# Feed-forward up-projections on TensorE: a high weight tile streams both parts of the activations in one matmul, and the first and last tiles get an order of their own

## The chip, the cores and the metric

The kernel runs on one core of a Trainium2 chip (eight cores in all, the other seven idle). The metric is the device time of one execution in microseconds; the number compared is the median of several executions.

## The reference, cut to what matters

The program is a chain of ten stages over 256 tokens of width 1024: a mixing layer, five feed-forwards and four other mixers. Only the feed-forwards change. Each is

```python
h = rmsnorm(x, g)                          # 256 x 1024
u = dwconv(h @ w_up, conv_w, conv_b)       # 256 x 5632, depthwise, 3 taps along the tokens
g, v = u[..., :D_FF], u[..., D_FF:]        # D_FF = 2816 = 22 tiles of 128
y = (gelu(g) * v) @ w_down                 # 256 x 1024
x = x + rmsnorm(y, g_post)
```

Everything is fp32. The kernel keeps this accuracy with two reduced fp32 parts of each operand, a high one (a copy in the type `F32R`) and a low one (the rest), and three products: high by high, low weight by high activation, high weight by low activation.

## The kernel before, in words

Weights arrive as one stream of 263 chunks of 128 x 2048 values (1 MB), in the order of use. SyncE loads chunk c into `raw`, a ring of 3 slots (`RING`), as soon as the low part of chunk c-3 has been made. ScalarE copies the chunk to `w_hi` (`split_hi`, L685, in the loop `loop_split`, L906) once TensorE has used chunk c-3; VectorE subtracts and writes `w_lo` (`split_lo`, L1171, in the loop L1491). TensorE waits for `lo_done`.

A feed-forward has 33 chunks: for each of 22 tiles of 128 inner channels an `up` chunk (gate and value columns of that tile, 8 blocks of 128 x 128 each), and for each pair of tiles one `down` chunk. The activations h lie transposed as 8 blocks of 128 x 256 in `h_hi` and `h_lo`.

TensorE (`ffn`, L2173): `up(t)` does 16 steps of three matmuls of 256 columns (`product`, L1988 to L1990) into one PSUM bank, gate in its left half and value in its right; three banks take turns. `down(i)` does 24 matmuls of 512 columns (L2086 to L2088) into the four banks 3 to 6, for the two tiles 2i and 2i+1. The order is up 0, up 1, up 2, up 3, down 0, then in a loop up 2i, up 2i+1, down i-1 for i = 2 to 10, and at the end down 10. During `up(1)` one more matmul (`root_row`, L1984) makes the row of inverse norms, which ScalarE copies to `rs_row` (L817).

VectorE does for each tile `up_norm` (L1450, bank times `rs_row` into `up_n`), four `taps` (L1464), `gated_value` (L1473) and `parts` (L1483 the high part, L1485 the low part of the product). ScalarE does for each tile two `centre` instructions (L894, the middle tap and the bias) and one `gelu` (L899). Both also split three chunks for each pair of tiles, and each engine works strictly in the order written. A tile passes back and forth: `up_norm` (VectorE), `centre` (ScalarE), `taps` (VectorE), `gelu` (ScalarE), `gated_value` and `parts` (VectorE), `down` (TensorE). The semaphores that matter are `chunk_used` (TensorE is through with a chunk), `lo_done` (its low part is there), `up_ready` (tile normalized), `ulo_done` (parts of the product are there). `up(t)` waits for `up_ready` of tile t-2, `down(i)` for `ulo_done` of its two tiles, one before each half of its matmuls.

The functions that the change touches:

## Time and profile before

| | us |
|---|---|
| median of 3 executions | 1613.67 (1613.43 to 1614.26) |
| the profiled execution | 1614.33, span 1612.5 |
| TensorE busy | 1591.2 (99% of the span) |
| VectorE busy | 1212.5 (75%) |
| ScalarE busy | 893.5 (55%) |
| GpSimd busy | 102.5 (6%) |
| DMA, share of 16 engines | 46.8% (main queue), mean 177 GB/s |

The span is the time from the first to the last recorded instruction of the profiled execution; 1.8 us of its own time lie around it. The share of busy time counts overlapping records once. A matmul's record is longer than the distance to the next one, since matmuls are pipelined: a busy share near 100% does not say how fast TensorE runs, the distance of two starts does, and a short wait between two matmuls can hide under the first one's record.

### The profile page before, as it was taken

How to read it: one execution, taken by the hardware profiler on the slowest of the kernel's cores; microseconds unless marked ns; L12 is line 12 of the kernel's file. 1: busy time of each engine (PE TensorE's matmuls, PEld its weight loads, DVE VectorE, ACT ScalarE, POOL GpSimd, SP SyncE). 2: the span in 40 equal slices, each digit the busy share in tenths (PEclk: the TensorE clock that was granted, in tenths of full speed). 3: DMA queues.
4: the chain of work that ended last, by engine and by line, in shares of the span. 5: the costliest groups of instructions: out<-in, count | busy, mean ns of one | idle time of the engine just before them, and what ended most of it. 6: DMA issues, size and time to landing. Idle time of an engine off the chain costs nothing.

```text
span 1612.5 us, 28655 instructions
## 1 busy us (share of the span) xinstructions
PE 1591.2 (99%) x10570; PEld 1440.4 (89%) x10570; DVE 1212.5 (75%) x1828; ACT 893.5 (55%) x1186; POOL 102.5 (6%) x110
## 2 busy tenths in 40 slices
PE   9999999999999999999999999999999999999999
PEld 8888999978899999869999998868999987899998
DVE  6757887778787877866887876456787887878787
ACT  6576554565655546665545555444645456664553
POOL 0031000000000001340000042000100000000000
PEclk9999999999999999999999999999999999999999
DMA  9435545443655454443554555524554545345443
GB/s 344 144 119 173 204 182 195 169 162 126 229 188 190 182 198 142 159 156 133 198 191 182 182 185 187 203 104 157 185 212 163 186 177 183 137 153 206 183 182 130
DMA packets 43394, 285.48 MB, mean 177 GB/s; under 512 B 5280, under 2 KB 5408, under 8 KB 10688
## 3 DMA queue, kind: packets, MB, share of 16 engines
q1 hardware_dynamic: 40592, 274.96, 46.8%
q0 software_dynamic: 2736, 9.60, 1.8%
q8 instruction: 46, 0.75, 0.2%
q14 instruction: 20, 0.16, 0.0%
HBM read 282.43 MB, written 1.05 MB: 176 GB/s over the span
## 4 chain that ended last, share of the span: by engine, by line
PE 91%; DVE 5%; issue 2%; ACT 1%; DMA 1%; SPq 0%; POOL 0%; DVEq 0%
PE bank L1988 16%; PE bank L1990 16%; PE bank L1989 16%; PE bank L2086 8%; PE bank L2087 8%; PE bank L2088 8%; PE bank L2036 4%; PE bank L2037 4%; PE bank L2038 4%; PE bank L1970 1%; PE bank L2485 1%; DVE w_lo L1171 1%; PE bank L2147 1%; DMA x<-x_in 1%; DVE w_lo L1491 0%
## 5 line engine op out<-in xcount | busy, mean ns | idle before, releaser
L1988 PE MATMUL bank<-h_hi,w_hi 128*128 128x256 f32 x2220 | 633.3, 285 | 5.4 <-issue 2.3
L1989 PE MATMUL bank<-h_hi,w_lo 128*128 128x256 f32 x2220 | 630.3, 284 | 0.0
L1990 PE MATMUL bank<-h_lo,w_hi 128*128 128x256 f32 x2220 | 630.2, 284 | 0.0
L1988 PEld LDWEIGHTS bank<-h_hi,w_hi 128*128 128x128 f32 x2220 | 425.5, 192 | 12.8 <-issue 8.6
L1989 PEld LDWEIGHTS bank<-h_hi,w_lo 128*128 128x128 f32 x2220 | 425.6, 192 | 3.0
L1990 PEld LDWEIGHTS bank<-h_lo,w_hi 128*128 128x128 f32 x2220 | 425.5, 192 | 0.8
L1491 DVE TENSOR_TENSOR w_lo<-raw,w_hi 128x2048 fp32r<-128x2048 f32 x145 | 327.5, 2284 | 3.9 <-ACT w_hi L906 3.9
L894 ACT ACTIVATE arena<-arena,par 128x256 f32<-128x256 f32 x220 | 120.3, 594 | 352.2 <-DVE arena L1450 348.9
L1171 DVE TENSOR_TENSOR w_lo<-raw,w_hi 128x2048 fp32r<-128x2048 f32 (+3 forms) x108 | 232.8, 2156 | 103.3 <-ACT w_hi L685 103.1
L906 ACT ACTIVATE w_hi<-raw 128x2048 fp32r<-128x2048 f32 x150 | 286.1, 1908 | 19.8 <-PE bank L2088 19.8
L2086 PE MATMUL bank<-w_hi,h_hi 128*128 128x512 f32 x632 | 248.2, 393 | 1.5 <-DVE h_lo L1485 1.5
L2087 PE MATMUL bank<-w_lo,h_hi 128*128 128x512 f32 x632 | 246.6, 390 | 0.0
L2088 PE MATMUL bank<-w_hi,h_lo 128*128 128x512 f32 x632 | 246.0, 389 | 0.0
L685 ACT ACTIVATE w_hi<-raw 128x2048 fp32r<-128x2048 f32 (+3 forms) x105 | 187.9, 1790 | 102.0 <-PE bank L2088 38.9
L1464 DVE SCALAR_TENSOR_TENSOR arena<-arena,par 128x255 f32<-128x255 f32 x440 | 183.2, 479 | 22.3 <-ACT arena L894 22.3
L1450 DVE TENSOR_TENSOR arena<-bank,rs_row 128x512 f32<-128x512 f32 x110 | 76.0, 691 | 117.2 <-PE bank L1990 110.3
L2086 PEld LDWEIGHTS bank<-w_hi,h_hi 128*128 128x128 f32 x632 | 118.9, 188 | 27.1 <-issue 3.7
L2088 PEld LDWEIGHTS bank<-w_hi,h_lo 128*128 128x128 f32 x632 | 118.7, 188 | 25.1
L2087 PEld LDWEIGHTS bank<-w_lo,h_hi 128*128 128x128 f32 x632 | 118.9, 188 | 22.6 <-issue 0.2
L2036 PE MATMUL bank<-w_hi,h_hi 128*128 128x512 f32 x308 | 120.8, 392 | 0.1
L2037 PE MATMUL bank<-w_lo,h_hi 128*128 128x512 f32 x308 | 119.9, 389 | 0.0
L2038 PE MATMUL bank<-w_hi,h_lo 128*128 128x512 f32 x308 | 119.9, 389 | 0.0
(231 smaller groups left out, 1318.7 us busy)
## 6 DMA issues: line engine op xcount, KB each, us to landing
raw<-wstream SPq DMA_DIRECT2D x252, 1024.0 KB, 4.8
raw<-wstream SPq DMA_DIRECT2D x8, 256.0 KB, 3.8
raw<-wstream SPq DMA_DIRECT2D x4, 512.0 KB, 7.6
arena<-dilated_bias POOLq DMA_DIRECT2D x8, 256.0 KB, 4.8
arena<-conv_rows POOLq DMA_DIRECT2D x2, 1024.0 KB, 4.9
arena<-window_bias POOLq DMA_DIRECT2D x4, 512.0 KB, 6.0
raw<-wstream SPq DMA_DIRECT2D x4, 384.0 KB, 3.4
cst<-consts SPq DMA_DIRECT2D x1, 1088.0 KB, 12.7
```

The source lines that it names most:

```text
L685: nc.scalar.activation(w_hi[:, c % RING, 0:w], raw[:, c % RING, 0:w], ACT.Copy).then_inc(hi_done, 1)
L906: nc.scalar.activation(w_hi[:, c % RING, :], raw[:, c % RING, :], ACT.Copy).then_inc(hi_done, 1)
L1171: nc.vector.tensor_tensor(w_lo[:, s, 0:w], raw[:, s, 0:w], w_hi[:, s, 0:w].bitcast(F32), ALU.subtract)\
L1491: nc.vector.tensor_tensor(w_lo[:, c % RING, :], raw[:, c % RING, :], w_hi[:, c % RING, :].bitcast(F32), ALU.subtract).then_inc(lo_done, 1)
L1988: nc.tensor.matmul(dst, w_parts[0], x_parts[0], start=start, stop=False, **kw)
L1989: nc.tensor.matmul(dst, w_parts[1], x_parts[0], start=False, stop=False, **kw)
L1990: return nc.tensor.matmul(dst, w_parts[0], x_parts[1], start=False, stop=stop, **kw)
L2036: nc.tensor.matmul(dst, a, w[0], start=not second and t == 0, stop=False, skip_group_check=True)
L2037: nc.tensor.matmul(dst, a, w[1], start=False, stop=False, skip_group_check=True)
L2086: nc.tensor.matmul(dst, hi, w[0], start=first and a == 0, stop=False, skip_group_check=True)
L2087: nc.tensor.matmul(dst, hi, w[1], start=False, stop=False, skip_group_check=True)
L2088: last = nc.tensor.matmul(dst, lo, w[0], start=False, stop=last_ and a == 1, skip_group_check=True)
```

## The change

Three things are changed in the feed-forwards.

1. `h_hi` and `h_lo` become two views of one buffer `h_both`, in which the high and low part of a block lie side by side (512 columns). The banks become one PSUM tensor, so that two neighbours can be read by one instruction (`up_banks`). In `up` a step is now two matmuls: the high weight with the high and low activations at once, 512 columns into a whole bank, and the low weight with the high activations, 256 columns into the bank's left half. A tile takes two banks, one for the gate and one for the value, and two pairs of banks take turns. `up(t)` waits for `up_sum` of tile t-2.
2. The left and the right half of each bank have to be added. ScalarE copies the right halves to `up_l` (`low_sums`, one instruction of 512 columns for a tile); VectorE adds them to the left halves and then multiplies by `rs_row` (`up_norm`, now two instructions). In exchange the high part of the product moves from VectorE (L1483) to ScalarE (`high_part`).
3. The first two pairs of tiles and the last pair are written out by hand on ScalarE and VectorE, in an order of their own; the loop covers i = 2 to 9 on both.

`root_row` of a feed-forward now writes to bank 3, since bank 7 belongs to a pair of `up` banks. The other stages only get the new addresses of `h_hi` and `h_lo` (two pieces of 256 columns where there was one of 512).

```diff
-        h_hi = sb("h_hi", [P, 16, S], F32R)
-        h_lo = sb("h_lo", [P, 16, S], F32R)
+        h_both = sb("h_both", [P, 16, 2, S], F32R)
+        h_hi, h_lo = h_both[:, :, 0, :], h_both[:, :, 1, :]
...
-        bank = [ctx.enter_context(nc.psum_tensor(f"bank{i}", [P, 512], F32)) for i in range(8)]
+        psum = ctx.enter_context(nc.psum_tensor("bank", [P, 8, 512], F32))
+        bank = [psum[:, (i + 1) % 8, :] for i in range(8)]
...
+        def up_banks(a):
+            return psum[:, 2 * a:2 * a + 2, :]
...
+                def low_sums(t, a, used):
+                    act.wait_ge(chunk_used, used)
+                    if not isinstance(t, int) or t >= 2:
+                        act.wait_ge(up_sum, t + (T0 - 1))
+                    nc.scalar.activation(halves(up_l[:, a, :]), up_banks(a)[:, :, S:2 * S], ACT.Copy).then_inc(up_low, 1)
+                def high_part(t, slot, used=None):
+                    act.wait_ge(prod_done, t + (T0 + 1))
+                    if used is not None:
+                        act.wait_ge(chunk_used, used)
+                    nc.scalar.activation(h_hi[:, slot, :], u32[:, slot % 2, :], ACT.Copy).then_inc(uhi_done, 1)
...
-                with act.Fori(1, FT // 2) as i:
-                    loop_split(i, 0)
-                    for a in range(2):
-                        centre(i * 2 + a, a)
-                        loop_split(i, 1 + a)
-                        gelu(i * 2 + a, a)
+                with act.Fori(2, FT // 2 - 1) as i:
+                    high_part(i * 2 + (-2), 8, i * 3 + (c0 - 1))
+                    loop_split(i, 0)
+                    high_part(i * 2 + (-1), 9, i * 3 + (c0 - 1))
+                    low_sums(i * 2, 0, i * 3 + c0)
+                    centre(i * 2, 0)
+                    loop_split(i, 1)
+                    low_sums(i * 2 + 1, 1, i * 3 + (c0 + 1))
+                    gelu(i * 2, 0)
+                    centre(i * 2 + 1, 1)
+                    loop_split(i, 2)
+                    gelu(i * 2 + 1, 1)
...
-                    dve.wait_ge(chunk_used, used)
+                    dve.wait_ge(up_low, t + (T0 + 1))
...
-                    nc.vector.tensor_tensor(halves(up_n[:, a, :]), halves(bank[bank_][:, :]),
+                    nc.vector.tensor_tensor(halves(up_n[:, a, :]), up_banks(a)[:, :, 0:S], halves(up_l[:, a, :]), ALU.add)\
+                             .then_inc(up_sum, 1)
+                    dve.wait_ge(up_sum, t + (T0 + 1))
+                    nc.vector.tensor_tensor(halves(up_n[:, a, :]), halves(up_n[:, a, :]),
                                             rs_row[:, :].unsqueeze(1).broadcast_to([P, 2, S]), ALU.mult).then_inc(up_ready, 1)
...
-                    for m in range(2):
-                        for kt in range(8):
-                            last = product(bank[slot_c % 3][:, m * S:(m + 1) * S], weights(slot_c, (8 * m + kt) * P),
-                                           h_parts(kt), kt == 0, kt == 7)
+                    for m, kt in steps:
+                        if wait_h is not None and m == 0:
+                            pe.wait_ge(hlo_done, wait_h + kt + 1)
+                        w, dst = weights(slot_c, (8 * m + kt) * P), up_banks(a)[:, m, :]
+                        nc.tensor.matmul(halves(dst), w[0], h_both[:, kt, :, :], start=kt == 0, stop=kt == 7, skip_group_check=True)
+                        last = nc.tensor.matmul(dst[:, 0:S], w[1], h_hi[:, kt, :], start=False, stop=kt == 7, skip_group_check=True)
```

How the instructions stand now. TensorE, four steps of an `up` around `root_row`, before (L1984 is `root_row`):

```order
L1988 MATMUL bank<-h_hi,w_hi 128x256
L1989 MATMUL bank<-h_hi,w_lo 128x256
L1990 MATMUL bank<-h_lo,w_hi 128x256
L1984 MATMUL bank<-hn,cst 128x256 [waits stat_read,root_diag]
L1988 MATMUL bank<-h_hi,w_hi 128x256
L1989 MATMUL bank<-h_hi,w_lo 128x256
L1990 MATMUL bank<-h_lo,w_hi 128x256
```

and now (L2055 is `root_row`, L2265 and L2266 are the step):

```order
L2265 MATMUL bank<-h_both,w_hi 128x512
L2266 MATMUL bank<-h_both,w_lo 128x256
L2055 MATMUL bank<-hn,cst 128x256 [waits stat_read,root_diag]
L2265 MATMUL bank<-h_both,w_hi 128x512
L2266 MATMUL bank<-h_both,w_lo 128x256
```

A step has two matmuls and two weight loads where it had three of each; `root_row` keeps its place after the eleventh step of `up(1)`.

VectorE at the start of a feed-forward, before (L1450 `up_norm`, L1464 `taps`, L1171 `split_lo`, L1473 `gated_value`, L1483 and L1485 `parts`):

```order
L1450 TENSOR_TENSOR arena<-bank,rs_row 128x512 [waits chunk_used,row_done]
L1450 TENSOR_TENSOR arena<-bank,rs_row 128x512 [waits chunk_used]
L1464 SCALAR_TENSOR_TENSOR arena<-arena,par 128x255 [waits lin_done] x2
L1464 SCALAR_TENSOR_TENSOR arena<-arena,par 128x255 [waits taps_done] x2
L1171 TENSOR_TENSOR w_lo<-raw,w_hi 128x2048 [waits hi_done]
L1464 SCALAR_TENSOR_TENSOR arena<-arena,par 128x255 [waits lin_done] x2
L1464 SCALAR_TENSOR_TENSOR arena<-arena,par 128x255 [waits taps_done] x2
L1473 TENSOR_TENSOR arena<-arena 128x256 [waits taps_done,gelu_done]
L1483 CAST h_hi<-arena 128x256 [waits chunk_used,prod_done]
L1485 TENSOR_TENSOR h_lo<-arena,h_hi 128x256 [waits uhi_done]
L1491 TENSOR_TENSOR w_lo<-raw,w_hi 128x2048 [waits hi_done]
```

and now (L1510 and L1513 `up_norm`, L1527 `taps`, L1230 `split_lo`, L1536 `gated_value`, L1541 `low_part`):

```order
L1510 TENSOR_TENSOR arena<-bank,arena 128x512 [waits up_low,row_done]
L1513 TENSOR_TENSOR arena<-arena,rs_row 128x512 [waits up_sum]
L1527 SCALAR_TENSOR_TENSOR arena<-arena,par 128x255 [waits lin_done] x2
L1527 SCALAR_TENSOR_TENSOR arena<-arena,par 128x255 [waits taps_done] x2
L1230 TENSOR_TENSOR w_lo<-raw,w_hi 128x2048 [waits hi_done]
L1510 TENSOR_TENSOR arena<-bank,arena 128x512 [waits up_low]
L1513 TENSOR_TENSOR arena<-arena,rs_row 128x512 [waits up_sum]
L1536 TENSOR_TENSOR arena<-arena 128x256 [waits taps_done,gelu_done]
L1527 SCALAR_TENSOR_TENSOR arena<-arena,par 128x255 [waits lin_done] x2
L1527 SCALAR_TENSOR_TENSOR arena<-arena,par 128x255 [waits taps_done] x2
L1230 TENSOR_TENSOR w_lo<-raw,w_hi 128x2048 [waits hi_done]
L1536 TENSOR_TENSOR arena<-arena 128x256 [waits taps_done,gelu_done]
```

The second tile's `up_norm` now stands behind the taps of the first tile and the low part of chunk 3, and the product's parts of both first tiles stand behind the low part of chunk 4 (L1541, next in the list).

ScalarE at the same place, now (L830 copies `rs_row`, L927 `low_sums`, L907 `centre`, L698 `split_hi`, L912 `gelu`, L934 `high_part`); before, the same list had no L927 and no L934, both `centre` pairs stood ahead of the table load with only one `split_hi` between them, and the second `split_hi` came after both `gelu`:

```order
L830 ACTIVATE rs_row<-bank 128x256 [waits row_sum]
L927 ACTIVATE arena<-bank 128x512 [waits chunk_used]
L907 ACTIVATE arena<-arena,par 128x256 [waits up_ready]
L907 ACTIVATE arena<-arena,par 128x256
L698 ACTIVATE w_hi<-raw 128x2048 [waits chunk_used,raw_full0]
L927 ACTIVATE arena<-bank 128x512 [waits chunk_used]
L912 ACT_TABLE_LOAD
L912 ACTIVATE arena<-arena 128x256 [waits taps_done]
L698 ACTIVATE w_hi<-raw 128x2048 [waits chunk_used,raw_full1]
L907 ACTIVATE arena<-arena,par 128x256 [waits up_ready]
L907 ACTIVATE arena<-arena,par 128x256
L934 ACTIVATE h_both<-arena 128x256 [waits chunk_used,prod_done]
```

The copy of the second tile's right halves waits behind the high part of chunk 3, and its `centre` behind the high part of chunk 4.

## Rows read from the trace of the kernel before

**Rows 1.** The page: busy time by engine; chain that ended last by engine.

```profile
PE 1591.2 (99%) x10570; PEld 1440.4 (89%) x10570; DVE 1212.5 (75%) x1828; ACT 893.5 (55%) x1186; POOL 102.5 (6%) x110
...
PE 91%; DVE 5%; issue 2%; ACT 1%; DMA 1%; SPq 0%; POOL 0%; DVEq 0%
```

**Rows 2.** Timeline of TensorE, end of the first feed-forward: start us, length us, line.

```profile
315.31 0.28 PE L1988 MATMUL bank<-h_hi,w_hi 128*128 128x256 f32 x1
...
318.79 0.28 PE L1990 MATMUL bank<-h_lo,w_hi 128*128 128x256 f32 x1
318.90 0.40 PE L2086 MATMUL bank<-w_hi,h_hi 128*128 128x512 f32 x1
...
320.07 0.39 PE L2088 MATMUL bank<-w_hi,h_lo 128*128 128x512 f32 x1
...
324.15 0.39 PE L2088 MATMUL bank<-w_hi,h_lo 128*128 128x512 f32 x1
324.83 0.47 PE L2086 MATMUL bank<-w_hi,h_hi 128*128 128x512 f32 x1 [0.30 <-DVE h_lo L1485]
325.14 0.40 PE L2087 MATMUL bank<-w_lo,h_hi 128*128 128x512 f32 x1
...
330.13 0.39 PE L2088 MATMUL bank<-w_hi,h_lo 128*128 128x512 f32 x1
```

**Rows 3.** Windows: 17 us inside the loop: length, busy us (xinstructions) by engine, clock, DMA.

```profile
204.00:221.00 17.00, 17.00 (x122) 16.04 (x121) 13.37 (x20) 8.46 (x10) 0.00 (x0) 1.00 0.49 185
```

**Rows 4.** Timeline of VectorE inside the loop, waits for TensorE in brackets.

```profile
229.16 0.41 DVE L1473 TENSOR_TENSOR arena<-arena 128x256 f32<-128x256 f32 x1
229.61 0.29 DVE L1483 CAST h_hi<-arena 128x256 fp32r<-128x256 f32 x1
229.93 0.43 DVE L1485 TENSOR_TENSOR h_lo<-arena,h_hi 128x256 fp32r<-128x256 f32 x1
230.82 1.67 DVE L1464 SCALAR_TENSOR_TENSOR arena<-arena,par 128x255 f32<-128x255 f32 x4 [0.46 <-ACT arena L894]
234.31 0.69 DVE L1450 TENSOR_TENSOR arena<-bank,rs_row 128x512 f32<-128x512 f32 x1 [1.82 <-PE bank L1990]
```

**Rows 5.** Groups of VectorE by shape: count, busy us, mean ns of one.

```profile
L1199 DVE TENSOR_TENSOR rs_t<-rs_y 128x512 f32<-128x512 f32 x8 | 5.5, 692 | 5.6 <-ACT rs_y L714 5.6
...
L1343 DVE TENSOR_TENSOR arena<-bank,sq 128x512 f32<-128x512 f32 x8 | 5.3, 688 | 6.6 <-ACT arena L827 6.6
```

**Rows 6.** Groups of ScalarE by shape.

```profile
L1015 ACT ACTIVATE h_hi<-arena 128x256 fp32r<-128x256 f32 x16 | 6.4, 421 | 6.6 <-DVE arena L1668 6.6
...
L1005 ACT ACTIVATE arena<-bank 128x512 f32<-128x512 f32 x12 | 6.3, 599 | 4.4 <-PE bank L2285 4.4
```

**Rows 7.** Timeline of TensorE, start of the first feed-forward.

```profile
142.24 0.36 PE L1988 MATMUL bank<-h_hi,w_hi 128*128 128x256 f32 x1
...
152.03 0.60 PE L1984 MATMUL bank<-hn,cst 128*128 128x256 f32 x2
```

**Rows 8.** Timeline of TensorE, where the first `up` of the loop begins.

```profile
171.01 0.39 PE L2088 MATMUL bank<-w_hi,h_lo 128*128 128x512 f32 x1
171.46 0.38 PE L1988 MATMUL bank<-h_hi,w_hi 128*128 128x256 f32 x1
```

**Rows 9.** Timeline of ScalarE, start of the first feed-forward.

```profile
152.66 0.39 ACT L817 ACTIVATE rs_row<-bank 128x256 f32<-128x256 f32 x1 [1.94 <-PE bank L1984]
153.81 1.09 ACT L894 ACTIVATE arena<-arena,par 128x256 f32<-128x256 f32 x2 [0.76 <-DVE arena L1450]
154.81 1.90 ACT L685 ACTIVATE w_hi<-raw 128x2048 fp32r<-128x2048 f32 x1
...
157.71 1.28 ACT L899 ACT_TABLE_LOAD   x1
```

**Rows 10.** Timeline of VectorE, start of the first feed-forward.

```profile
149.24 2.29 DVE L1171 TENSOR_TENSOR w_lo<-raw,w_hi 128x2048 fp32r<-128x2048 f32 x1 [0.73 <-ACT w_hi L685]
153.08 0.69 DVE L1450 TENSOR_TENSOR arena<-bank,rs_row 128x512 f32<-128x512 f32 x1 [1.54 <-ACT rs_row L817]
```

More of the change, by code:

```diff
@@ L440, in build_program @@
         xs = region(2560, 2, D)
+        up_l = region(2560, 2, 512)
         glu_in = region(0, 2, 512)
@@ L772, in x_squares, with prenorm @@
                     nc.scalar.activation(xs_piece(q), x_piece(q), ACT.Square, accum_out=sum_at(q)).then_inc(piece_sq, 1)
-            def prenorm(c0, gain, by_row=True, then=None, columns=False):
+            def prenorm(c0, gain, by_row=True, then=None, columns=False, row=stat):
                 if c0:
@@ L813, in prenorm @@
                 act.wait_ge(row_sum, k["row"])
-                src, dst = stat[:, 0:S], rs_row[:, :]
+                src, dst = row[:, 0:S], rs_row[:, :]
                 if columns:
@@ new lines, in ffn @@
+                split_hi(c0 + 5)
+                high_part(1, 9, c0 + 2)
+                centre(2, 0)
+                low_sums(3, 1, c0 + 4)
+                split_hi(c0 + 6)
+                gelu(2, 0)
+                centre(3, 1)
+                gelu(3, 1)
+                with act.Fori(2, FT // 2 - 1) as i:
+                    high_part(i * 2 + (-2), 8, i * 3 + (c0 - 1))
+                    loop_split(i, 0)
+                    high_part(i * 2 + (-1), 9, i * 3 + (c0 - 1))
[7 more added lines that the diff above has]
+                    gelu(i * 2 + 1, 1)
@@ new lines, in ffn @@
+                high_part(FT - 4, 8, c0 + 29)
+                split_hi(c0 + 31)
+                high_part(FT - 3, 9, c0 + 29)
+                low_sums(FT - 2, 0, c0 + 30)
+                centre(FT - 2, 0)
+                split_hi(c0 + 32)
+                gelu(FT - 2, 0)
+                low_sums(FT - 1, 1, c0 + 31)
+                high_part(FT - 2, 10)
+                centre(FT - 1, 1)
+                split_hi(c0 + 33)
+                gelu(FT - 1, 1)
+                high_part(FT - 1, 11)
@@ L1494, in ffn @@
                 prenorm(gain, c0)
-                up_norm(0, 0, c0 % 3, c0 + 1)
-                up_norm(1, 1, (c0 + 1) % 3, c0 + 2)
+                up_norm(0, 0)
                 taps(0, 0)
                 split_lo(c0 + 3)
+                up_norm(1, 1)
+                gated_value(0, 0)
                 taps(1, 1)
-                gated_value(0, 0)
-                def two_tiles(i):
-                    used = i * 3 + (c0 - 1)
-                    parts(i * 2 + (-2), 0, used)
-                    if not isinstance(i, int):
-                        loop_split(i, -1)
+                split_lo(c0 + 4)
+                gated_value(1, 1)
+                low_part(0, 8)
+                low_part(1, 9)
+                up_norm(2, 0)
+                split_lo(c0 + 5)
+                taps(2, 0)
+                up_norm(3, 1)
+                gated_value(2, 0)
+                taps(3, 1)
+                with dve.Fori(2, FT // 2 - 1) as i:
+                    loop_split(i, -1)
+                    gated_value(i * 2 + (-1), 1)
+                    low_part(i * 2 + (-2), 8)
+                    low_part(i * 2 + (-1), 9)
+                    up_norm(i * 2, 0)
                     loop_split(i, 0)
-                    up_norm(i * 2, 0, (c0 + 2) % 3, i * 3 + c0)
-                    gated_value(i * 2 + (-1), 1)
-                    parts(i * 2 + (-1), 1, used)
                     taps(i * 2, 0)
-                    up_norm(i * 2 + 1, 1, (c0 + 3) % 3, i * 3 + (c0 + 1))
+                    up_norm(i * 2 + 1, 1)
                     loop_split(i, 1)
@@ L1515, in two_tiles @@
                     taps(i * 2 + 1, 1)
-                two_tiles(1)
-                with dve.Fori(2, FT // 2) as i:
-                    two_tiles(i)
-                parts(FT - 2, 0)
+                split_lo(c0 + 30)
+                gated_value(FT - 3, 1)
+                low_part(FT - 4, 8)
+                low_part(FT - 3, 9)
+                up_norm(FT - 2, 0)
+                split_lo(c0 + 31)
+                taps(FT - 2, 0)
+                gated_value(FT - 2, 0)
+                up_norm(FT - 1, 1)
+                low_part(FT - 2, 10)
+                split_lo(c0 + 32)
+                taps(FT - 1, 1)
                 gated_value(FT - 1, 1)
-                parts(FT - 1, 1)
+                low_part(FT - 1, 11)
                 split_lo(c0 + 33)
```

87 lines of the change are left out of this document (46 added, 41 removed).

## The prediction, made before the changed kernel was run

> **What bounds the kernel now.** I read the page first, then the chain of waits. TensorE is on 91% of the chain that ended last, VectorE on 5% [rows 1]. So whatever shortens TensorE's own stream shortens the kernel, until another engine is late. Busy time does not give the size of that: a record of 256 columns is 0.28 us long, but the next one starts 0.12 us later. I therefore took distances of starts from TensorE's timeline [rows 2]. From 315.31 to 318.79 lie 29 distances of 256-column matmuls, 3.48 us, so 0.120 us each. From 318.90 to 324.15 lie 23 distances of 512-column matmuls, 0.2283 each, and from 325.14 to 330.13 another 22, 0.2268 each; I take 0.2275. The difference, 0.1075 us for 256 columns, is 2.4 GHz, and the granted clock is 1.00 [rows 3]. What does not scale with columns is 0.120 - 0.1075 = 0.0125 us: each matmul with a weight tile of its own pays it, short or long.
>
> Inside the loop a pair of tiles costs 96 x 0.120 + 24 x 0.2275 = 16.98 us. In a window of 17.00 us TensorE has no idle time, VectorE is busy for 13.37, ScalarE for 8.46, DMA at a share of 0.49 [rows 3]. VectorE's longest wait there is 1.82 us for TensorE [rows 4]. TensorE sets the pace, and the others have 3.6 and 8.5 us to spare. At the edges it is closer. `up 4` starts 0.45 us after the matmul ahead of it instead of 0.23 [rows 8]. The second half of the last `down` starts 0.68 us after the first half's last matmul instead of 0.23, and the next distance is 0.31, so about 0.5 us are lost there [rows 2].
>
> **The stream.** A step was 3 x 0.120 = 0.360 us. It becomes 0.2275 + 0.120 = 0.3475, so 0.0125 less: the columns are the same 768, one fixed cost is gone. With 16 steps, 22 tiles and 5 feed-forwards that is 1760 x 0.0125 = 22.0 us, 4.4 for each feed-forward. No row shows a 512-column matmul and a 256-column one taking turns; the bounds are below. The Trainium skill ("TensorE: Matmul & The Clock Gate", section "Back-to-back issue gap") gives the distance of warm matmuls as N/2.4 + 2.5 ns; by that the fixed cost would be 2.5 ns and the whole saving only 1760 x 0.0025 = 4.4 us. The rows above speak against it here.
>
> **The loop on the other engines.** VectorE gives up two casts of 0.29 us for each pair of tiles [rows 4] and gets two additions from PSUM and SBUF, 0.69 each by the nearest row, L1343. The old `up_norm` keeps its 0.69 though it now reads SBUF (L1199, 0.69) [rows 5]. 13.37 - 0.6 + 1.4 = 14.2 us. ScalarE gets two `low_sums`, 0.60 each (L1005), and two high parts, 0.42 each (L1015) [rows 6]: 8.46 + 2.0 = 10.5 us. The new pace of TensorE is 32 x 0.3475 + 24 x 0.2275 = 16.58 us. Both fit, VectorE with 2.4 us of slack. The chain for one tile also fits: `up(t+2)` needs `up_sum(t)` one `up` and one `down` later in most cases, about 11 us, against 1.3 us of work and at most one 1.90 us split ahead of it. So in the loop nothing is lost. The move of the casts is free there: it hides under ScalarE's idle time, and would cost 0.42 us for each tile without it. The weight loads wait for `lo_done` of three chunks earlier; splitting one takes 1.9 + 2.3 us [rows 9, 10] of the 16 us of three chunks, with the DMA queue at 0.49 [rows 3].
>
> **The start.** Here the two banks are missed: `up 2` needs the first pair of banks back right after `up 1`, and there is no `down` yet to give time. I walk through the first feed-forward with the old durations. All five start alike, so I multiply by five.
> - TensorE starts at 142.24 as before [rows 7]. 16 steps take 5.56, and `root_row`, 27 steps in, comes at 151.6, 0.4 earlier than the old 152.03; `up 1` ends at 153.6.
> - ScalarE ends the copy of `rs_row` at 152.65 (old 153.05, minus 0.4) [rows 9]. `low_sums` 0 ends at 153.2, the sum of tile 0 on VectorE at 153.9. TensorE starts about 0.15 after a release, so `up 2` starts at 154.1: **0.5 lost**.
> - The multiplication ends at 154.5, `centre` 0 (1.09 for two) at 155.6, the high part of chunk 3 (1.90) at 157.5 [rows 9], its low part (2.29) [rows 10] at 159.8, the sum of tile 1 behind it at 160.4. `up 2` ended at 159.65, `up 3` starts at 160.6: **0.9 lost**.
> - ScalarE: `low_sums` 1 to 158.0, table load (1.28) to 159.2, `gelu` 0 to 159.6, high part of chunk 4 to 161.4, `centre` 1 to 162.4. VectorE: taps (1.67) to 164.2, low part of chunk 4 to 166.4, gated value (0.41) to 166.8, low part of product 0 (0.43) to 167.2, of product 1 to 167.7 [rows 4]. `up 3` ended at 166.15, `down 0` starts at 167.4: **1.3 lost**.
> - VectorE goes on with sum and product of tile 2 to 168.9, low part of chunk 5 to 171.1, taps to 172.7, tile 3's sum and product to 173.9, its taps (after `centre` 3) from 175.2 to 176.9, low part of chunk 6 to 179.1. TensorE ended `down 0` at 172.9 and `up 4` at 178.4, and starts `up 5` at 179.3: **0.9 lost**. After that VectorE gains 2.4 us for each pair of tiles, and the delays end.
>
> Sum 3.6 us, minus the 0.3 of `up 4` before: 3.3 us more for each feed-forward.
>
> **The end.** `low_part(20)` and `gated_value(20)` now stand ahead of the low part of chunk 32, and the last tile's `gated_value` directly behind its taps, where two instructions of tile 20 stood between. The same walk has the last product ready when the second half of `down 10` is due, within 0.1 us. So about 0.4 to 0.5 of the 0.5 us come back. The post-norm's table load and squares follow at the same distance.
>
> **Other stages.** Address changes alone: same counts, columns and types. I price them at nothing; the work they would hide behind is TensorE's, and 0.01 us on each of their few hundred instructions off the chain stays unseen.
>
> **Sum.** For each feed-forward -4.4 + 3.3 - 0.5 = -1.6 us; five give -8. The profiled execution took 1614.3, so 1606.3; its time is 0.66 above the median, so I forecast a median of 1605.7, 0.5% less. A measurement of this kernel can tell about 0.2%, 3.2 us, from no change. The four waits at the start are the weak term: 0.2 us more or less on the chain through ScalarE and VectorE for each of them is 0.8 x 5 = 4 us. That gives 1601 to 1611 for this case.
>
> **Rivals.**
> - *The fixed cost does not vanish with the matmul (slower).* The first five distances of a `down` are (320.07 - 318.90) / 5 = 0.234 us [rows 2], more than the mean. If a 512-column matmul behind a 256-column one always costs that, a step is 0.354 and saves 0.006: 10.6 us, against 14 us of net waits at the edges (5 x 2.8): 1617. It decides below 14 / 1760 = 0.008 us for a step. By the page's 2.5 ns the time would be 1613.7 - 4.4 + 14 = 1623. Against it: the later distances are 0.227, whatever came before. Chance 0.14, of it 0.05 within 0.2%.
> - *The start does not wait.* If the copy, the sum and the splits of the first tiles overlap better than I walked, only the gain is left: -22 - 2.5 gives 1589, and half the waits 1597. For it: each wait is about 1 us and rests on four or five durations. Against it: the same walk, made for the old order, gives waits of 0.5 us at `up 4` and 0.7 at the end where the rows show 0.3 and 0.5 [rows 2, 8]. Chance 0.12.
> - *Mixed matmuls run closer still.* Where 256 columns are followed by 512 the distance is 0.11 (318.79 to 318.90) [rows 2]. A step of 0.3375 saves 39.6 us, of which the waits at the start, where TensorE arrives earlier, take some 17: 1591. One distance at two decimals bears it. Chance 0.06.
> - *VectorE becomes the bound in the loop (slower).* It needs 2.4 us more than I count, 0.15 on each of 16 to 17 instructions. At 1 us beyond, 9 pairs of tiles and 5 feed-forwards cost 45 us, some 1640. Chance 0.04.
> - *It does not do what it says*: the gain in the stream and the waits cancel for a reason I do not see, 1613.7. Chance 0.04.
>
> **The numbers.** My case has 0.60, of which 0.04 lies within 0.2%. Faster: 0.56 + 0.12 + 0.06 = 0.74. Same: 0.04 + 0.05 + 0.04 = 0.13. Slower: 0.09 + 0.04 = 0.13. The range from 1592 to 1615 takes in my case, half or more of the waits gone, part of the closer stream and everything that cancels; it leaves out about 2 in 10.
>
> **What would show it.** Starts in an `up` 0.2275 and 0.120 apart in turn, an `up` of 5.56 us and a period in the loop of 16.6 us: the stream. VectorE at 14.2 us in such a period, with waits left: the loop. `up 2`, `up 3`, `down 0` and `up 5` held by 0.5, 0.9, 1.3 and 0.9 us, the first two after `up_norm`'s sum: the start. The last `down` without its gap: the end. I am wrong if the period is above 16.8, if TensorE waits inside the loop, or if the start's waits sum to under 2 or over 5 us.

## The result and the profile after

| | before | after |
|---|---|---|
| median | 1613.93 us (20 runs, 1613.26 to 1615.44) | 1616.53 us (20 runs, 1616.03 to 1617.15 and one of 1669.20) |
| ratio, 95% interval | | 1.0016 [1.0009, 1.0022] |
| profiled execution, its span | 1614.3, 1612.5 | 1617.15, 1615.2 |

The change makes the kernel 2.6 us slower (0.16%), where I had forecast a gain of 8 us. The interval excludes 1. The one execution of 1669.20 us ran at a lower granted clock (0.897) and is left out of the ratio.

The page of the kernel after answers to [rows 1]: busy time by engine, then the chain that ended last. VectorE is now on 12% of that chain instead of 5%, ScalarE on 5% instead of 1%.

```profile
PE 1582.5 (98%) x8810; PEld 1346.6 (83%) x8810; DVE 1248.4 (77%) x1828; ACT 995.1 (62%) x1406; POOL 102.4 (6%) x110
...
PE 79%; DVE 12%; ACT 5%; issue 3%; DMA 1%; SPq 0%; POOL 0%; DVEq 0%
```

TensorE's timeline inside the loop shows the new step (start us, length us, line; L2265 is the 512-column matmul, L2266 the 256-column one):

```profile
224.74 0.28 PE L2266 MATMUL bank<-h_both,w_lo 128*128 128x256 f32 x1
224.85 0.40 PE L2265 MATMUL bank<-h_both,w_hi 128*128 128x512 f32 x1
225.09 0.28 PE L2266 MATMUL bank<-h_both,w_lo 128*128 128x256 f32 x1
225.21 0.40 PE L2265 MATMUL bank<-h_both,w_hi 128*128 128x512 f32 x1
225.45 0.28 PE L2266 MATMUL bank<-h_both,w_lo 128*128 128x256 f32 x1
225.56 0.40 PE L2265 MATMUL bank<-h_both,w_hi 128*128 128x512 f32 x1
```

From 224.85 to 225.56 lie two steps, 0.71 us. Averaged over the 32 steps of two `up`, it takes 0.236 us from a 512-column matmul to the next start, not 0.2275, and 0.117 from a 256-column one, not 0.120. The 32 steps take 11.29 us, 0.353 for a step; before it was 11.51, and forecast was 11.12.

The window of one period of the loop answers to [rows 3]: length, then busy us of TensorE, weight loads, VectorE, ScalarE and GpSimd, the granted clock, the DMA share. TensorE never stands idle in it. VectorE has 13.96 us of work (forecast 14.2), ScalarE 10.35 (10.5). The period is 16.79 us against 16.98 before and 16.58 forecast.

```profile
224.85:241.64 16.79, 16.79 (x90) 14.30 (x89) 13.96 (x20) 10.35 (x13) 0.00 (x0) 1.00 0.51 187
```

TensorE's timeline at the start of the first feed-forward shows the waits: `up 2`, `up 3`, `down 0` and `up 5`. The matmul ahead of the first stands above it.

```profile
154.09 0.28 PE L2266 MATMUL bank<-h_both,w_lo 128*128 128x256 f32 x1
154.48 0.47 PE L2265 MATMUL bank<-h_both,w_hi 128*128 128x512 f32 x1
...
161.07 0.47 PE L2265 MATMUL bank<-h_both,w_hi 128*128 128x512 f32 x1 [0.81 <-DVE arena L1510]
...
167.72 0.47 PE L2162 MATMUL bank<-w_hi,h_both 128*128 128x512 f32 x1 [0.76 <-DVE h_both L1541]
...
179.67 0.50 PE L2265 MATMUL bank<-h_both,w_hi 128*128 128x512 f32 x1 [0.62 <-DVE w_lo L1547]
```

These four (the first is the one at 154.48) start 0.39, 1.08, 1.04 and 0.89 us after the matmul ahead of each, instead of the usual 0.117: 0.3, 1.0, 0.9 and 0.8 us are lost.

**Where the time went.** I measured each feed-forward from its first `up` to its last matmul. The first one splits into three parts:

| us | before | after | difference | forecast |
|---|---|---|---|---|
| first `up` to the loop's first `down` | 40.82 | 43.02 | +2.20 | +2.1 |
| 8 periods of the loop | 135.84 | 134.34 | -1.50 | -3.2 |
| last two `down` (48 matmuls) | 11.23 | 10.72 | -0.51 | -0.5 |
| sum | 187.89 | 188.08 | +0.19 | -1.6 |

All five together take 939.46 us before and 939.72 after: the parts up to the loop 10.45 us more, the loops 7.6 less, the ends 2.6 less. So the feed-forwards themselves come out even, and some 2.4 us lie outside them. Nearly all of them are at the seams behind the feed-forwards. VectorE's timeline at the end of the program shows it; L1230 is the low part of the next chunk, L1389 the residual adds (L1171 and L1330 before the change).

```profile
1606.48 0.43 DVE L1536 TENSOR_TENSOR arena<-arena 128x256 f32<-128x256 f32 x1
1607.39 0.42 DVE L1541 TENSOR_TENSOR h_both<-arena,h_both 128x256 fp32r<-128x256 f32 x1 [0.48 <-ACT h_both L934]
1607.73 2.29 DVE L1230 TENSOR_TENSOR w_lo<-raw,w_hi 128x2048 fp32r<-128x2048 f32 x1
1609.93 2.47 DVE L1389 TENSOR_TENSOR x<-x,bank 128x512 f32<-128x512 f32 x4
```

The same stretch of the kernel before:

```profile
1604.41 2.28 DVE L1171 TENSOR_TENSOR w_lo<-raw,w_hi 128x2048 fp32r<-128x2048 f32 x1
1607.23 2.73 DVE L1330 TENSOR_TENSOR x<-x,bank 128x512 f32<-128x512 f32 x4 [0.54 <-PE bank L2088]
```

Before, the adds waited for the matmuls. Now they wait for nothing but VectorE, and come late: from the start of the last matmul to the end of the span it takes 4.59 us (1610.61 to 1615.2) instead of 3.66 (1608.84 to 1612.5), 0.93 more. The seam after the second feed-forward is the same case. The last matmul starts at 619.08, and the one that turns `x` 0.66 us later; before, it started 0.23 us later (618.65, 618.88). With three such seams, 1.3 us. VectorE's rows there are those of the program's end again, first before the change, then after it:

```profile
617.03 2.73 DVE L1330 TENSOR_TENSOR x<-x,bank 128x512 f32<-128x512 f32 x4 [0.52 <-PE bank L2088]
```

```profile
616.20 2.29 DVE L1230 TENSOR_TENSOR w_lo<-raw,w_hi 128x2048 fp32r<-128x2048 f32 x1
618.40 2.48 DVE L1389 TENSOR_TENSOR x<-x,bank 128x512 f32<-128x512 f32 x4
```

TensorE's row for the turn:

```profile
619.08 0.39 PE L2164 MATMUL bank<-w_hi,h_both 128*128 128x512 f32 x1
619.74 2.29 PE L2041 MATMUL bank<-cst,x 128*128 128x128 f32 x16 [0.27 <-DVE x L1389]
```

### The profile page after: what moved, and what is told of

Same layout as the page of the kernel before. It is cut to its first block, busy times and chain, and to the rows that moved or that the text cites. A ratio compares the mean times of both kernels' runs of the same rounds, so it can differ in the third digit from the quotient of the medians.

```text
span 1615.2 us, 25361 instructions
## 1 busy us (share of the span) xinstructions
PE 1582.5 (98%) x8810; PEld 1346.6 (83%) x8810; DVE 1248.4 (77%) x1828; ACT 995.1 (62%) x1406; POOL 102.4 (6%) x110
## 4 chain that ended last, share of the span: by engine, by line
PE 79%; DVE 12%; ACT 5%; issue 3%; DMA 1%; SPq 0%; POOL 0%; DVEq 0%
PE bank L2265 21%; PE bank L2266 10%; PE bank L2162 7%; PE bank L2164 7%; PE bank L2163 7%; PE bank L2112 4%; PE bank L2114 4%; PE bank L2113 4%; DVE w_lo L1230 4%; PE bank L2059 3%; PE bank L2060 2%; PE bank L2061 2%; DVE arena L1527 2%; DVE arena L1513 1%; DVE arena L1510 1%
## 5 line engine op out<-in xcount | busy, mean ns | idle before, releaser
L2265 PE MATMUL bank<-h_both,w_hi 128*128 128x512 f32 x1760 | 625.4, 399 | 8.1 <-DVE arena L1510 3.8
L2266 PE MATMUL bank<-h_both,w_lo 128*128 128x256 f32 x1760 | 493.6, 280 | 0.0
L2265 PEld LDWEIGHTS bank<-h_both,w_hi 128*128 128x128 f32 x1760 | 330.6, 188 | 93.2 <-issue 7.1
L1230 DVE TENSOR_TENSOR w_lo<-raw,w_hi 128x2048 fp32r<-128x2048 f32 (+3 forms) x133 | 289.9, 2180 | 103.8 <-ACT w_hi L698 103.1
L2266 PEld LDWEIGHTS bank<-h_both,w_lo 128*128 128x128 f32 x1760 | 332.3, 189 | 1.9
L698 ACT ACTIVATE w_hi<-raw 128x2048 fp32r<-128x2048 f32 (+3 forms) x135 | 245.0, 1815 | 100.2 <-PE bank L2164 37.3
L1547 DVE TENSOR_TENSOR w_lo<-raw,w_hi 128x2048 fp32r<-128x2048 f32 x120 | 274.1, 2284 | 0.0
L2162 PE MATMUL bank<-w_hi,h_both 128*128 128x512 f32 x632 | 249.1, 394 | 4.0 <-DVE h_both L1541 4.0
L2164 PE MATMUL bank<-w_hi,h_both 128*128 128x512 f32 x632 | 246.8, 391 | 0.0
L2163 PE MATMUL bank<-w_lo,h_both 128*128 128x512 f32 x632 | 246.3, 390 | 0.0
L907 ACT ACTIVATE arena<-arena,par 128x256 f32<-128x256 f32 x220 | 120.4, 595 | 168.2 <-DVE arena L1513 168.2
L1527 DVE SCALAR_TENSOR_TENSOR arena<-arena,par 128x255 f32<-128x255 f32 x440 | 183.1, 478 | 15.2 <-ACT arena L907 15.2
L1510 DVE TENSOR_TENSOR arena<-bank,arena 128x512 f32<-128x512 f32 x110 | 75.9, 690 | 111.5 <-ACT arena L927 110.7
L2162 PEld LDWEIGHTS bank<-w_hi,h_both 128*128 128x128 f32 x632 | 118.6, 188 | 31.0 <-DVE w_lo L1230 5.5
L2164 PEld LDWEIGHTS bank<-w_hi,h_both 128*128 128x128 f32 x632 | 118.6, 188 | 26.2
L2163 PEld LDWEIGHTS bank<-w_lo,h_both 128*128 128x128 f32 x632 | 118.8, 188 | 23.4 <-issue 0.2
L2059 PE MATMUL bank<-h_both,w_hi 128*128 128x256 f32 (+1 forms) x460 | 133.7, 291 | 4.4 <-issue 2.3
L2060 PE MATMUL bank<-h_both,w_lo 128*128 128x256 f32 (+1 forms) x460 | 132.3, 288 | 0.0
L2061 PE MATMUL bank<-h_both,w_hi 128*128 128x256 f32 (+1 forms) x460 | 132.2, 287 | 0.0
L2112 PE MATMUL bank<-w_hi,h_both 128*128 128x512 f32 x308 | 120.8, 392 | 0.0
L2113 PE MATMUL bank<-w_lo,h_both 128*128 128x512 f32 x308 | 119.9, 389 | 0.0
```

Source lines behind the costliest of these rows:

```text
L698: nc.scalar.activation(w_hi[:, c % RING, 0:w], raw[:, c % RING, 0:w], ACT.Copy).then_inc(hi_done, 1)
L1230: nc.vector.tensor_tensor(w_lo[:, s, 0:w], raw[:, s, 0:w], w_hi[:, s, 0:w].bitcast(F32), ALU.subtract)\
L1527: nc.vector.scalar_tensor_tensor(o, i_, par[:, bass.ds(t * 8 + (pb + 4 * w + tap), 1)], o, ALU.mult, ALU.add).then_inc(taps_done, 1)
L1547: nc.vector.tensor_tensor(w_lo[:, c % RING, :], raw[:, c % RING, :], w_hi[:, c % RING, :].bitcast(F32), ALU.subtract).then_inc(lo_done, 1)
L2112: nc.tensor.matmul(dst, a, w[0], start=not second and t == 0, stop=False, skip_group_check=True)
L2113: nc.tensor.matmul(dst, a, w[1], start=False, stop=False, skip_group_check=True)
```

## The experiments

Three theories, one for each part. Each run is compared with the kernel after the change; its ratio is to the kernel before, run beside it. **A**: the step saves less than forecast because a 512-column and a 256-column matmul take turns. Its rival: the new address pattern of the moving operand (two pieces of 256) costs it. **S**: the waits at a feed-forward's start come from when the row reaches ScalarE and VectorE, and from idle VectorE time ahead of the taps. Its rival: VectorE is full there. **V**: the seams are late because one split stands ahead of the residual adds.

**x1_three**: the new layout and order, with the old three matmuls of 256 columns.

```
-    matmul(halves(dst), w[0], h_both[:, kt, :, :], ...)
-    matmul(dst[:, 0:S], w[1], h_hi[:, kt, :], ...)
+    matmul(dst[:, 0:S], w[0], h_hi[:, kt, :], ...)
+    matmul(dst[:, 0:S], w[1], h_hi[:, kt, :], ...)
+    matmul(dst[:, S:2 * S], w[0], h_lo[:, kt, :], ...)
```

> Undoes the stream alone: three matmuls of 256 columns for a step again, all else (two banks for a tile, low_sums, the new orders) as in the change. Theory A (a step of 512 + 256 columns costs 0.353 us, only 0.007 less than three of 256, because the fixed cost grows when long and short matmuls take turns): an up goes back from 5.65 to 5.76 us and its down from 5.50 to 5.47, so about 9 to 11 us slower than the change, near 1626. Rival B (the stream gave the 0.0125 us of my forecast and something else ate it): 20 us or more slower, near 1637. Either way the waits at the start of a feed-forward stay near 3 us each time.

Measured: 1625.47 us, ratio 1.0072 [1.0055, 1.0089]. So streaming both parts is worth 8.9 us (1625.47 - 1616.53), and everything else in the change costs 11.6 (1625.47 - 1613.86, the median of before beside it). The two `up` of a period take 11.51 us again, as before the change.

**x2_flat**: the same 512 columns written as one flat row instead of two pieces.

```
-    matmul(halves(dst), w[0], h_both[:, kt, :, :], ...)
+    matmul(dst, w[0], flat(h_both[:, kt, :, :]), ...)
```

> The 512-column matmul is written with plain rows of 512 values on both sides instead of two pieces of 256. Theory A: nothing changes, the step stays at 0.353 us and the time within 1 us of the change. Rival C (the two-piece address pattern costs the 5 ns): the step falls to 0.348 us, 1760 x 0.005 = 9 us faster, near 1608.

Measured: 1616.55 us, ratio 1.0017 [1.0007, 1.0026], the same as the kernel after. This run tests less than I meant: the two pieces of 256 lie side by side in `h_both`, and the trace records the moving operand of L2265 as one row of 512 in the kernel after already, as it does here. So there never was a two-piece pattern on the reading side of this step. The rival falls all the same, since the slow steps are there with a flat row.

**x3_group16**: the same 32 matmuls in each `up`, the sixteen of 512 columns first, then the sixteen of 256.

```
+    for part in range(2):
         for m, kt in steps:
...
+            if part == 0:
                 matmul(halves(dst), w[0], h_both[:, kt, :, :], ...)
+            else:
                 last = matmul(dst[:, 0:S], w[1], h_hi[:, kt, :], ...)
```

> In each up all 16 matmuls of 512 columns come first, then all 16 of 256: the same matmuls and weight loads, two switches of length for a tile instead of 32. Theory A (alternating costs 5 ns for a step): the 512s come 0.2275 us apart after the first few at 0.234, the 256s 0.120; an up takes 5.58 to 5.62 us instead of 5.65, 3 to 8 us less in all. Rival C (address pattern, or the reading of h_both): the distance of the 512s stays at 0.234 or more and the up at 5.65. The first up of a feed-forward now needs all eight h tiles early and may wait a little more.

Measured: 1602.1 us, ratio 0.9925 [0.9908, 0.9942]: 14.4 us less than the kernel after, where I had expected 3 to 8. TensorE's timeline, where equal matmuls follow each other and stand as one row:

```profile
189.13 3.79 PE L2268 MATMUL bank<-h_both,w_hi 128*128 128x512 f32 x16
192.76 2.08 PE L2272 MATMUL bank<-h_both,w_lo 128*128 128x256 f32 x16
194.67 0.63 PE L2268 MATMUL bank<-h_both,w_hi 128*128 128x512 f32 x2
```

Sixteen of 512 take 3.63 us, 0.227 each; sixteen of 256 take 1.91, 0.119 each. A step is 0.3465 us, about what the forecast had (0.3475). That explains 352 x 0.0065 = 2.3 us of each feed-forward, 11.4 in all. The feed-forwards together take 924.07 us, 15.65 less than after. (Between two of them, from 710 to 713 us of this profiled execution, the granted clock is 0.50, which takes back some 1.7 us, an estimate from half the rate over 3.4 us.) The rest is at the start: `root_row` stands at the same step of the list, and it now comes after 11 matmuls of `up 1` instead of 22.

```profile
150.36 0.59 PE L2055 MATMUL bank<-hn,cst 128*128 128x256 f32 x2
```

It runs at 150.36 us instead of 152.04, and `up 2` and `up 3` no longer wait; `down 0` and `up 5` still wait 0.84 and 0.71 us. I had changed two things with one edit.

**x4_group2**: groups of two steps, so two of 512 columns, then two of 256. `root_row` stays where it was.

```
+    for group in [steps[j:j + 2] for j in range(0, 16, 2)]:
+        for part in range(2):
+            for m, kt in group:
```

> Two matmuls of 512, then two of 256, in turn: half as many switches. Theory A in its plain form (a price for each switch): half of the 5 ns, an up of 5.61 us, some 4 us less than the change. If the cost fades only over five or more matmuls, as the first distances of a down suggest (0.234, later 0.227), it stays at 5.65.

Measured: 1607.74 us, ratio 0.9963 [0.9949, 0.9977], 8.8 us less than after.

```profile
190.19 0.61 PE L2268 MATMUL bank<-h_both,w_hi 128*128 128x512 f32 x2
190.64 0.40 PE L2272 MATMUL bank<-h_both,w_lo 128*128 128x256 f32 x2
190.87 0.63 PE L2268 MATMUL bank<-h_both,w_hi 128*128 128x512 f32 x2
191.34 0.39 PE L2272 MATMUL bank<-h_both,w_lo 128*128 128x256 f32 x2
191.57 0.63 PE L2268 MATMUL bank<-h_both,w_hi 128*128 128x512 f32 x2
```

Two steps take 0.70 us (190.87 to 191.57), the two `up` of a period 11.13 us, so a step 0.348, and the period of the loop is 16.59. The waits at the start are there (1.18, 1.23 and 1.09 us from the start of the pair ahead, where 0.23 is usual), so this run shows the stream alone: 8 periods by 0.2 us and five feed-forwards are 8.1 of the 8.8 us. The same matmuls on the same operands run, and only their order changed. That shows **A** as far as this: the extra cost comes from mixing the two lengths in turn.

It does not show a price for each change of length, and my expectation missed in both its forms (half of the cost back, or none of it). With half as many changes as the kernel after, nearly all of what x3 gained in the stream came back: two `up` take 11.29 us after, 11.13 here and 11.11 with one group of sixteen. Nor does a distance depend on its two neighbours alone. Here a pair of 512 takes 0.466 us from its start to the next pair's and a pair of 256 takes 0.231, while in x3 the distances at the two changes of length are 0.226 and 0.120, no more than in a uniform run. What x3 and the kernel before show is a slow start of a run: the first five distances of 512 behind sixteen or more matmuls of 256 are 0.232 to 0.234 on average, the later ones 0.227.

**x5_early_row**: the kernel after, with `root_row` earlier.

```
-    if between and (m, kt) == (1, 2):
+    if between and (m, kt) == (0, 1):
```

> The kernel after the change, with one difference: the matmul of the root row (root_row, L2055) is issued in up(1) after its second step instead of after its eleventh. In the kernel after, VectorE has written its input at 148.7 us, the matmul runs at 152.04, and ScalarE is free from 150.9. Theory S (the waits at a feed-forward's start come from the time at which ScalarE and VectorE get the row): the copy of the row starts near 150.9 instead of 152.67, everything behind it on both engines moves forward by some 1.7 us, the waits of up(2) (0.4 us) and up(3) (1.1 us) go, and those of down(0) and up(5) stay at 0.8 and 0.7 us or a little less, since VectorE is the one that is full there. 1.3 to 1.8 us in each of five feed-forwards: 1607.5 to 1610 us. Rival E (the waits come from the order of the instructions on VectorE alone, whatever the time of the row): no change, 1615.5 to 1617.

Measured: 1608.74 us, ratio 0.9969 [0.9957, 0.998], 7.8 us less than after. In the timeline of TensorE the waits of `up 2` and `up 3` are gone, and these two are left:

```profile
164.84 0.48 PE L2162 MATMUL bank<-w_hi,h_both 128*128 128x512 f32 x1 [0.43 <-DVE h_both L1541]
...
176.80 0.50 PE L2265 MATMUL bank<-h_both,w_hi 128*128 128x512 f32 x1 [0.57 <-DVE w_lo L1547]
```

The time of the row is one half of **S**. It is also what x3 had mixed in; there the row came at 150.36 us, here at 147.87, and there it gave some 4 us (15.65 - 11.4).

**x6_start_order**: as x5, and the first splits fill the idle time ahead of the first taps.

```
 ScalarE
     low_sums(0, 0, c0 + 1)
-    centre(0, 0)
     split_hi(c0 + 3)
+    centre(0, 0)
     low_sums(1, 1, c0 + 2)
-    gelu(0, 0)
     split_hi(c0 + 4)
+    gelu(0, 0)
...
 VectorE
     up_norm(0, 0)
-    taps(0, 0)
     split_lo(c0 + 3)
+    taps(0, 0)
     up_norm(1, 1)
     gated_value(0, 0)
-    taps(1, 1)
     split_lo(c0 + 4)
+    taps(1, 1)
```

> As the early row, and with another order at a feed-forward's start: ScalarE makes the high part of chunk 3 before it centres tile 0, and that of chunk 4 and the low sums of tile 2 a place earlier; VectorE makes the low part of chunk 3 before the taps of tile 0, and that of chunk 4 before the taps of tile 1. Theory S with an idle VectorE (VectorE stood idle 1.16 and 1.04 us in front of the taps of tiles 0 and 1, and these two are what down(0) and up(5) wait for): all waits at the start but those of the old kernel go, some 3.3 us in each of five feed-forwards: 1599 to 1602 us, with no gap over 0.3 us before down(0) and up(5). Rival (VectorE is full from the row to down(0), whatever the order): the time of the early row alone.

Measured: 1601.9 us, ratio 0.9926 [0.991, 0.9943], 14.6 us less than after. No wait for VectorE or ScalarE is left at the start of the first feed-forward, and TensorE's list of waits names none of VectorE's L1510, L1541 and L1547 any more. VectorE's timeline there has one idle stretch of 0.32 us between the row and the taps of tile 1:

```profile
152.37 2.29 DVE L1230 TENSOR_TENSOR w_lo<-raw,w_hi 128x2048 fp32r<-128x2048 f32 x1 [0.32 <-ACT w_hi L698]
154.57 1.67 DVE L1527 SCALAR_TENSOR_TENSOR arena<-arena,par 128x255 f32<-128x255 f32 x4
156.16 0.69 DVE L1510 TENSOR_TENSOR arena<-bank,arena 128x512 f32<-128x512 f32 x1
```

The kernel after stood idle 1.16 and 1.04 us ahead of the taps of tiles 0 and 1:

```profile
156.22 1.67 DVE L1527 SCALAR_TENSOR_TENSOR arena<-arena,par 128x255 f32<-128x255 f32 x4 [1.16 <-ACT arena L907]
...
163.03 1.67 DVE L1527 SCALAR_TENSOR_TENSOR arena<-arena,par 128x255 f32<-128x255 f32 x4 [1.04 <-ACT arena L907]
```

The five feed-forwards take 924.69 us, 15.0 less. **S** holds in full: the waits at the start cost 15 us, and all of them came from order, none from too much work.

**x7_pool_end**: the low part of the next chunk, at a feed-forward's end, on GpSimd.

```
 GpSimd, at the end of a feed-forward
+    low_parts(c0 + 33, 512)
 VectorE
     low_part(FT - 1, 11)
-    split_lo(c0 + 33)
```

> The kernel after the change, with one difference: at a feed-forward's end the low part of the next chunk (w_lo, 128x2048) is made by GpSimd in four pieces of 128x512 (1.27 us each elsewhere in this kernel) instead of by VectorE, 2.28 us. Theory V (what the change gives back at the end is that VectorE comes late to the residual adds behind that instruction): the adds start right behind the sums that they read, the matmuls that turn x wait 0.2 us instead of 0.66 three times, and from the last matmul to the end of the span it takes 3.7 us or less instead of 4.59: 1613.5 to 1615 us. Rival P (GpSimd takes time from VectorE beside it, and the last two down chunks wait for the low part of tile 21): a gap of over 0.3 us in the last down chunk and 1616.5 us or more.

Measured: 1643.11 us, ratio 1.0186 [1.0169, 1.0203], 26.6 us more than after. The rival holds (it said 1616.5 or more and a gap of over 0.3 us), and by far more than I had thought; theory V is not tested by this run. GpSimd, VectorE and TensorE at the end of the first feed-forward:

```profile
324.14 5.70 POOL L601 TENSOR_TENSOR w_lo<-raw,w_hi 128x512 fp32r<-128x512 f32 x4 [182.81 <-ACT w_hi L700]
```

```profile
323.56 3.75 DVE L1529 SCALAR_TENSOR_TENSOR arena<-arena,par 128x255 f32<-128x255 f32 x4
327.40 1.31 DVE L1538 TENSOR_TENSOR arena<-arena 128x256 f32<-128x256 f32 x1
329.20 0.92 DVE L1543 TENSOR_TENSOR h_both<-arena,h_both 128x256 fp32r<-128x256 f32 x1 [0.48 <-ACT h_both L936]
```

```profile
330.17 0.50 PE L2163 MATMUL bank<-w_hi,h_both 128*128 128x512 f32 x1 [3.05 <-DVE h_both L1543]
```

Beside GpSimd, VectorE's four taps take 3.75 us instead of 1.67, its product 1.31 instead of 0.42, its difference 0.92 instead of 0.42. GpSimd's own pieces take 1.43 instead of 1.27. TensorE waits 3.05 us for the last low part. The list of TensorE's waits (us in total, times, longest) has 19.2 us on VectorE's last low parts over the program, of which 4.0 at `down 0` were in the kernel after already and 15.2 are new, and 5.3 us for `conv_rows`, a load that GpSimd issues behind the four pieces:

```profile
PE bank L2163 <- DVE h_both L1543: 19.2, 10, 3.1
PE bank L2113 <- DMA arena<-conv_rows: 5.3, 2, 3.2
```

That is 20.5 of the 26.6 us. Most of the rest is TensorE's clock. Four times the granted clock falls from 1.00 to 0.50 (from 2.4 to 1.2 GHz) for 3.4 us, three times behind the 3 us of idle time and once behind a row of shorter ones (0.68, 0.96 and 2.13 us); 512-column matmuls then start 0.43 us apart instead of 0.23. At half the rate that is 6.8 us, an estimate. The second such place:

```profile
626.09 0.79 PE L2163 MATMUL bank<-w_hi,h_both 128*128 128x512 f32 x1 [3.06 <-DVE h_both L1543]
626.68 0.63 PE L2164 MATMUL bank<-w_lo,h_both 128*128 128x512 f32 x1
627.11 0.63 PE L2165 MATMUL bank<-w_hi,h_both 128*128 128x512 f32 x1
```

The Trainium skill ("SBUF — State Buffer", section "SBUF: two separate sides") says that VectorE instructions with two SBUF inputs and GpSimd instructions lock each other out of a shared pair of ports for a whole instruction. The trace agrees in kind: each of VectorE's instructions there has two SBUF inputs and becomes longer by one GpSimd piece (1.43 us) or less; single taps take 0.48 to 1.52 us.

**x8_best**: grouping, early row, start order and GpSimd together.

> All in one: each up's sixteen matmuls of 512 columns ahead of its sixteen of 256, the row after the fifth of up(1)'s matmuls, the start order, and GpSimd for the low part at the end. Grouped matmuls alone gave 1602.1 us, and still waited 0.84 and 0.71 us before down(0) and up(5), 1.6 us in each of five feed-forwards; with these gone and 2 us less at the ends: 1591 to 1594 us. If GpSimd disturbs VectorE: 1594 to 1598.

Measured: 1616.57 us, ratio 1.0016 [1.0006, 1.0025], outside both ranges that I had given (1591 to 1598). GpSimd at the end takes back all that the rest gains: `down 10` waits 3.2 us in each feed-forward, and the granted clock is 0.50 for some 20 us in all, each time behind 3.2 to 3.6 us of idle time. x10 is the same without it, and without the split of the unread chunk.

**x9_no_filler**: the kernel after, without the split of the stream's last chunk, which nothing reads.

```
-    if c >= n_chunks or c in second_chunks and not second:
+    if c >= n_chunks - 1 or c in second_chunks and not second:
```

> The kernel after the change, without the high and the low part of the last chunk of the stream, which fills the ring and which no matmul reads (1.90 us on ScalarE, 2.28 us on VectorE). Theory V (VectorE comes late to the residual adds since this instruction is ahead of them): the adds start when their sums are there, as in the kernel before, and from the last matmul to the end of the span it takes 3.7 us instead of 4.59: 0.9 us less, 1615.6 us. Rival (the adds wait for the matmuls in any case, and the 0.9 us come from elsewhere): no change, and 4.6 us from the last matmul to the end.

Measured: 1616.13 us, ratio 1.0015 [1.0006, 1.0024]. The time does not resolve 0.9 us. The trace does: VectorE waits for TensorE again ahead of the adds, as before the change.

```profile
1607.20 0.42 DVE L1541 TENSOR_TENSOR h_both<-arena,h_both 128x256 fp32r<-128x256 f32 x1 [0.49 <-ACT h_both L934]
1608.81 2.73 DVE L1389 TENSOR_TENSOR x<-x,bank 128x512 f32<-128x512 f32 x4 [1.18 <-PE bank L2164]
```

From the start of the last matmul (1610.42) to the end of the span (1614.1) it takes 3.68 us, forecast 3.7. **V** is shown for the end of the program. For the three seams inside it, it is argued from the same rows of VectorE (617.03 before, 616.20 and 618.40 after); there the split is needed, and its one relocation that I tried, x7, made things worse.

**x10_best**: grouping by `up`, the row after the fifth matmul of `up 1`, the start order, no split of the unread chunk.

> The matmuls of 512 and of 256 columns grouped by up (a step of 0.3465 us instead of 0.353: 352 steps by 0.0065, 2.3 us in each of five feed-forwards), the early row and the start order (measured together 1601.9 us), and no parts of the unread chunk (0.9). If the terms add up: 1601.9 - 11.5 - 0.9 = 1589.5 us, 1588.5 to 1592. If the shorter loop brings a new wait (VectorE has 0.2 to 0.5 us to spare before the last down chunk): 1592 to 1596, with gaps before the down chunks.

Measured: 1589.72 us, ratio 0.9853 [0.9838, 0.9868], 26.8 us less than after and 24 less than before. The terms add up, inside the range of 1588.5 to 1592. The feed-forwards take 913.42 us, 26.3 less than after. The wait at a seam has grown a little (L2041 on L1389: 1.2 us in three, after 0.8). This version beats both kernels, by 1.5% of the time before.

## Why the prediction was wrong

The forecast was -8 us, the measurement +2.6; between them are 10.6 us. Two steps failed.

- **The stream: the step that failed.** "It becomes 0.2275 + 0.120 = 0.3475, so 0.0125 less." Measured 0.353, so 0.007 less. The two prices were right for runs of equal matmuls, as x3 shows, and wrong for taking turns. In the loop each period came out 0.19 us shorter instead of 0.40: over 8 periods and five feed-forwards 8.4 us, most of the miss. The rival "the fixed cost does not vanish with the matmul" had the price (0.354), the row it came from (the first distances of a `down`, [rows 2]) and the time (1617). That it came so close is in part luck: its row is not a mixed one either, since those five distances lie between matmuls of 512 that follow a run of 256, and the seams, which it leaves out, make up for waits that came out shorter. I spoke against it with the later distances of 0.227, "whatever came before". They come after five or more of their own length and say nothing on a mixed stream. No row of the trace showed one; the distance of 0.11 at the one change of length in [rows 2] is a single distance, and the run that goes with it costs more.
- **The seams: left out.** "The post-norm's table load and squares follow at the same distance", and nothing on the four feed-forwards that end in residual adds. The order at the end brings tile 21's parts later on VectorE, and with them the split ahead of the adds. The seams cost 0.93 + 1.3 = 2.2 us. With the 8.4 of the stream that is 10.6, the whole difference.
- **The start: right in its mechanism, its total by luck.** Forecast waits of 0.5, 0.9, 1.3 and 0.9 us, measured 0.3, 1.0, 0.9 and 0.8, at the four places and for the reasons named. That is 3.0 us instead of 3.6. The part up to the loop still came out 2.2 us longer, against 2.1 forecast, because its six `up` gave 0.5 us less than forecast: two misses that cancel, 2.6 to 3 us each over five feed-forwards. `root_row` did not come 0.4 us earlier (152.04 against 152.03 before), since the steps ahead of it were longer than forecast and the stage began 0.17 later. That the row's time sets the waits was implied in the walk, not drawn out; x5 and x6 show that the whole term could be had back.
- **The loop on the other engines: right.** 13.96 and 10.35 us of work in a period, no wait of TensorE.
- **The end: right for TensorE.** 0.51 us came back; on VectorE see above.
- **Other stages: right**, as far as the rows tell. Where they read two pieces of 256 now (L2059 to L2061), the distance is 0.227 us, as it was for one piece of 512 before. x2 does not bear on this.
- **The signs of being wrong: too wide.** None of the three came. The period had to be above 16.8 and was 16.79, yet 16.79 instead of 16.58 alone is 8.4 us, the whole forecast gain.
- **The rule weighed there.** The Trainium skill ("TensorE: Matmul & The Clock Gate", section "Back-to-back issue gap") has a fixed cost of 2.5 ns, for an isolated matmul, which gave 1623 with my waits. The runs do not agree with it: 256 columns after 256 cost 0.0125 us beyond their columns here.

What stays open: why a mixed stream costs TensorE time, and why pairs are enough to avoid most of it. The runs exclude the address pattern (a flat row of 512 in the trace of the kernel after and of x2). The `down` chunks exclude the alternation of high and low weights, since they alternate them too at 0.227 us, and they exclude reading the same activations twice in a row, since they do that as well. A row of matmuls on one bank is the same in all the orders.

## What to carry to other kernels

Merging two short matmuls into a long one saves only the fixed cost, and here a stream that then alternates long and short gave half of it back. Issue equal lengths in groups; two in a row were enough for most of it. When a buffer is handed back by a chain over two engines, look at when the chain's first input is issued and at idle time behind it, before you call an engine full. A term is to be read from rows of the same stream: the mean of a uniform stream does not price a mixed one, and neither does one distance at the change. And set the sign of being wrong where it would catch half of the gain: a bound on a period is multiplied by all periods.
